# Routing of a mixture of experts: fewer candidate sums, and key numbers picked by compare-and-multiply steps

## What is computed

```python
s1 = einsum('thd,kd->thk', q[:, :, 0], sub_k1)      # scores of 128 keys, first half
s2 = einsum('thd,kd->thk', q[:, :, 1], sub_k2)      # second half
v1, i1 = top_k(s1, 16)
v2, i2 = top_k(s2, 16)
cand = v1[..., :, None] + v2[..., None, :]          # 16 x 16 sums
cand_idx = i1[..., :, None] * 128 + i2[..., None, :]
top_s, top_pos = top_k(cand, 16)
eidx = take_along_axis(cand_idx, top_pos)           # 16 experts of 16384
gate = softmax(top_s)
act = gelu(einsum('thkd,td->thk', expert_u[eidx], x))
y = einsum('thk,thkd->td', gate * act, expert_v[eidx])
```

## Time and profile before

| | us |
|---|---|
| median of 3 runs | 3937.94 |
| the three runs | 3937.94, 3937.79, 3953.55 |
| the profiled execution | 3934.07 |
| its span, from the first to the last instruction | 3932.2 |
| PE busy | 3654.2 |
| DVE busy | 2497.1 |
| POOL busy | 1856.5 |
| ACT busy | 1357.9 |

### The profile page before, as it was taken

One profiled execution on the slowest core, in us unless ns is written; L12 is line 12 of the kernel. 1 busy time (PEld: TensorE's weight loads), 2 busy tenths in 40 slices (PEclk: granted clock), 3 DMA queues, 4 the chain that ended last, 5 costly groups with the idle time before them and its releaser, 6 DMA issues.

```text
span 3932.2 us, 62108 instructions
## 1 busy us (share of the span) xinstructions
PE 3654.2 (93%) x21581; PEld 3445.0 (88%) x21581; DVE 2497.1 (64%) x5088; ACT 1357.9 (35%) x1905; POOL 1856.5 (47%) x1120
## 2 busy tenths in 40 slices
PE   7799999998999999999888599999999999999998
PEld 7799999898999999998853357899898989999998
DVE  2341187878785777775556531287878785777774
ACT  3222244444444333333221233243434444333332
POOL 3333475565555555553520001466555655555551
PEclk9899999999999999999998799999999999999999
DMA  3122266777778999983245131256777788999992
GB/s 119 65 71 75 86 189 221 253 247 256 251 274 274 310 309 318 327 281 99 65 123 174 45 100 49 75 178 215 237 260 240 260 267 294 294 311 318 322 311 101
DMA packets 380008, 812.58 MB, mean 207 GB/s; under 512 B 33544, under 2 KB 239304, under 8 KB 372552
## 3 DMA queue, kind: packets, MB, share of 16 engines
q1 hardware_dynamic: 167024, 464.17, 35.2%
q0 software_dynamic: 61072, 221.08, 16.5%
q10 hardware_dynamic: 151696, 124.51, 10.7%
HBM read 696.90 MB, written 112.74 MB: 206 GB/s over the span
## 4 chain that ended last, share of the span: by engine, by line
PE 68%; DVE 19%; DMA 5%; issue 3%; ACT 2%; POOL 2%; ACTq 0%; SPq 0%; DVEq 0%; POOLq 0%
PE acc L566 39%; PE acc L553 15%; PE misc L697 4%; DMA rows<-u_in,expertP 3%; DVE rows L1626 3%; PE misc L920 2%; DVE hot L1558 1%; DVE hot L1564 1%; POOL w_lo L2039 1%; PE acc L934 1%; DMA raw<-slabs_in 1%; DVE hot_gate L1664 1%; DVE route L1569 1%; DVE work L1521 1%; DVE keyi L1529 1%
## 5 line engine op out<-in xcount | busy, mean ns | idle before, releaser
L2039 POOL TENSOR_TENSOR w_lo<-raw,w_hi 128x1024 fp32r<-128x1024 f32 x368 | 920.1, 2502 | 1349.4 <-ACT w_hi L1015 1348.1
L566 PE MATMUL acc<-h_hi,w_hi 128*128 128x416 f32 x3072 | 1101.5, 359 | 10.4 <-POOL w_lo L2039 9.2
L566 PE MATMUL acc<-h_lo,w_hi 128*128 128x416 f32 x3072 | 1088.6, 354 | 0.0
L566 PE MATMUL acc<-h_hi,w_lo 128*128 128x416 f32 x3072 | 1083.7, 353 | 0.0
L1015 ACT ACTIVATE w_hi<-raw 128x1024 fp32r<-128x1024 f32 x620 | 656.1, 1059 | 1166.1 <-DMA raw<-slabs_in 1134.8
L566 PEld LDWEIGHTS acc<-h_hi,w_hi 128*128 128x128 f32 x3072 | 583.9, 190 | 21.1 <-ACT gelu L1125 11.9
L566 PEld LDWEIGHTS acc<-h_hi,w_lo 128*128 128x128 f32 x3072 | 583.8, 190 | 7.5
L566 PEld LDWEIGHTS acc<-h_lo,w_hi 128*128 128x128 f32 x3072 | 583.5, 190 | 4.2
L1743 DVE TENSOR_TENSOR w_lo<-raw,w_hi 128x1024 fp32r<-128x1024 f32 x252 | 330.8, 1313 | 202.0 <-ACT w_hi L1015 201.6
L1626 DVE CUSTOM_DVE_ANT_0 rows<-acc,rows 128x1024 f32<-128x1024 f32 (+1 forms) x224 | 273.6, 1222 | 226.5 <-DMA rows<-u_in,expertP 182.6
L553 PE MATMUL acc<-h_hi,w_hi 128*128 128x260 f32 x1472 | 308.3, 291 | 78.9 <-DVE h_lo L1433 30.3
(11 more groups left out here) (319 smaller groups left out, 5340.2 us busy)
## 6 DMA issues: line engine op xcount, KB each, us to landing
raw<-slabs_in SPq DMA_DIRECT2D x620, 512.0 KB
act_d<-gelu SPq DMA_DIRECT2D x256, 208.0 KB
gate_d<-gout SPq DMA_DIRECT2D x52, 1024.0 KB
abuf<-act_d ACTq DMA_DIRECT2D x32, 1664.0 KB
gbuf<-gate_d ACTq DMA_DIRECT2D x30, 1664.0 KB
unit<-cv_in SPq DMA_DIRECT2D x128, 128.0 KB, 2.0
unit<-ck_in SPq DMA_DIRECT2D x64, 160.0 KB, 2.9
unit<-ck_in ACTq DMA_DIRECT2D x64, 160.0 KB, 3.2
```

Source lines behind the costliest of these rows:

```text
L566: last = pe.matmul(acc[:, 0, par, 0:ND], w[:, c, :], m(c), start=c == 0 and w is w_hi[r] and m is m_hi, stop=c == KC - 1 and w is w_lo[r])
L2039: pool.tensor_tensor(w_lo[r][:], raw[r][:], w_hi[r][:].bitcast(F32), ALU.subtract).then_inc(lo_done, 1)
```

## The change

Of the 256 sums of a sorted list of 16 with a sorted list of 16, the greatest 16 have either their first place or their second below 4. So 112 sums are kept: the first 4 keys of side one with all 16 of side two (64), and the other 12 with the first 4 (48). They are made by two additions. The place in this list no longer gives the two key places by a shift and a mask, so they are worked out by arithmetic on small float tiles (`rowf`, with five rows in place of two). The key numbers were picked by comparing with 0 to 15, multiplying and summing over 2048 elements for each side; now for each k of 0 to 15 one instruction compares the places with k and multiplies with the number of key k, for both sides in one, and an addition sums it up. The places and the partial picks lie in PSUM (`misc` banks 3 and 2) for the prompt blocks and in SBUF for the sample tokens. `between()` is still called 12 times.

```diff
+EDGE = 4
+PAIRS = EDGE * TOPK + (TOPK - EDGE) * EDGE
...
-        cand = at("cand", [P, PH, TOPK, TOPK], F32, sc_at)
-        cwork = at("cwork", [P, PH, TOPK * TOPK], F32, work_at)
-        hot = at("hot", [P, PH, TOPK, TOPK], F32, work_at)
+        cand = at("cand", [P, PH, PAIRS], F32, sc_at)
+        cwork = at("cwork", [P, PH, PAIRS], F32, work_at)
...
-                dve.tensor_copy(kf[0:w], ki[0:w]).then_inc(dve_step, step.up())
+                dve.tensor_copy(kf[0:w].rearrange("p (s h) k -> p s h k", s=2),
+                                ki[0:w].rearrange("p (h s) k -> p s h k", s=2)).then_inc(dve_step, step.up())
...
-                dve.tensor_tensor(sums[0:w], best[:, 0].unsqueeze(3).to_broadcast([w, heads, TOPK, TOPK]),
-                                  best[:, 1].unsqueeze(2).to_broadcast([w, heads, TOPK, TOPK]), ALU.add).then_inc(
-                    dve_step, step.up())
+                for lo, hi, n, first in ((0, EDGE, TOPK, 0), (EDGE, TOPK, EDGE, EDGE * TOPK)):
+                    each = [w, heads, hi - lo, n]
+                    dve.tensor_tensor(sums[0:w, :, first:first + (hi - lo) * n].rearrange("p h (a b) -> p h a b", b=n),
+                                      best[:, 0, :, lo:hi].unsqueeze(3).to_broadcast(each),
+                                      best[:, 1, :, 0:n].unsqueeze(2).to_broadcast(each), ALU.add).then_inc(
+                        dve_step, step.up())
...
-                dve.tensor_scalar(rw[0:w, 1], tp[0:w], 15, None, ALU.bitwise_and).then_inc(dve_step, step.up())
+                dve.tensor_scalar(rw[0:w, 1], tp[0:w], 2, None, ALU.logical_shift_right).then_inc(dve_step, step.up())
+                dve.tensor_copy(rwf[0:w, 2], tp[0:w]).then_inc(dve_step, step.up())
                 dve.wait_ge(dve_step, step.at)
-                dve.tensor_copy(rwf[0:w], rw[0:w]).then_inc(dve_step, step.up())
+                dve.tensor_copy(rwf[0:w, 0:2], rw[0:w]).then_inc(dve_step, step.up())
                 dve.wait_ge(dve_step, step.at)
-                numbers = kf[0:w].rearrange("p (h s) k -> p s h k", s=2)
-                for s in range(2):
-
-                    dve.tensor_tensor(pick[0:w].rearrange("p h k a -> p (h k) a"),
-                                      rwf[0:w, s].rearrange("p h k -> p (h k)").unsqueeze(2).to_broadcast(
-                                          [w, heads * TOPK, TOPK]),
-                                      iota[0:w, 0:TOPK].unsqueeze(1).to_broadcast([w, heads * TOPK, TOPK]),
-                                      ALU.is_equal).then_inc(dve_step, step.up())
+
+                dve.scalar_tensor_tensor(rwf[0:w, 3], rwf[0:w, 1], float(-(TOPK - EDGE)), rwf[0:w, 0], ALU.add,
+                                         ALU.max).then_inc(dve_step, step.up())
+                dve.wait_ge(dve_step, step.at)
+                dve.tensor_copy(place[0:w, 0], rwf[0:w, 3]).then_inc(dve_step, step.up())
+                dve.scalar_tensor_tensor(rwf[0:w, 0], rwf[0:w, 3], float(-TOPK), rwf[0:w, 2], ALU.mult,
+                                         ALU.add).then_inc(dve_step, step.up())
+                dve.scalar_tensor_tensor(rwf[0:w, 1], rwf[0:w, 3], float(-EDGE), rwf[0:w, 2], ALU.mult,
+                                         ALU.add).then_inc(dve_step, step.up())
+                dve.wait_ge(dve_step, step.at)
+                dve.scalar_tensor_tensor(place[0:w, 1], rwf[0:w, 1], float(-EDGE * (TOPK - EDGE)), rwf[0:w, 0], ALU.add,
+                                         ALU.max).then_inc(dve_step, step.up())
+                dve.wait_ge(dve_step, step.at)
+                between()
+                both = [w, 2 * heads, TOPK]
+                flat = lambda t: t.rearrange("p s h k -> p (s h) k")
+                for k in range(TOPK):
+                    to = flat(pick[0:w] if k else out[0:w, 0:2])
+                    dve.scalar_tensor_tensor(to, flat(place[0:w]), float(k), kf[0:w, :, k:k + 1].to_broadcast(both),
+                                             ALU.is_equal, ALU.mult).then_inc(dve_step, step.up())
                     dve.wait_ge(dve_step, step.at)
-                    dve.tensor_tensor(pick[0:w], pick[0:w],
-                                      numbers[:, s].unsqueeze(2).to_broadcast([w, heads, TOPK, TOPK]),
-                                      ALU.mult).then_inc(dve_step, step.up())
-                    dve.wait_ge(dve_step, step.at)
-                    between()
-                    dve.tensor_reduce(out[0:w, s], pick[0:w], AX, ALU.add).then_inc(dve_step, step.up())
-                    dve.wait_ge(dve_step, step.at)
-                    between()
+                    if k:
+                        dve.tensor_tensor(out[0:w, 0:2], pick[0:w], out[0:w, 0:2], ALU.add).then_inc(dve_step, step.up())
+                        dve.wait_ge(dve_step, step.at)
+                    if k % 6 == 5:
+                        between()
+                between()
...
+            place = misc[:, 3, P:P + 2 * SLOTS].rearrange("p (s h k) -> p s h k", s=2, h=PH)
+            pick = misc[:, 2, 0:2 * SLOTS].rearrange("p (s h k) -> p s h k", s=2, h=PH)
```

More of the change, by code:

```diff
@@ L211, in build @@
         row = take("row", [P, 2, PH, TOPK], U32)
-        rowf = take("rowf", [P, 2, PH, TOPK])
+        rowf = at("rowf", [P, 5, PH, TOPK], F32, work_at + 4096)
         route = take("route", [P, 3, PH, TOPK])
@@ L221, in build @@
         rowS = take("rowS", [P, 2, 1, TOPK], U32)
-        rowfS = take("rowfS", [P, 2, 1, TOPK])
+        rowfS = take("rowfS", [P, 5, 1, TOPK])
         routeS = take("routeS", [P, 3, 1, TOPK])
@@ L245, in build @@
         scS = at("scS", [P, 2, P], F32, s_at)
-        candS = at("candS", [P, 1, TOPK, TOPK], F32, s_at)
+        candS = at("candS", [P, 1, PAIRS], F32, s_at)
         workS = at("workS", [P, 2, P], F32, s_at + 1024)
-        cworkS = at("cworkS", [P, 1, TOPK * TOPK], F32, s_at + 1024)
-        hotS = at("hotS", [P, 1, TOPK, TOPK], F32, s_at + 1024)
+        cworkS = at("cworkS", [P, 1, PAIRS], F32, s_at + 1024)
+        placeS = at("placeS", [P, 2, 1, TOPK], F32, s_at + 1024)
+        pickS = at("pickS", [P, 2, 1, TOPK], F32, s_at + 1536)
         take = region()
@@ L1531, in top16, with chosen @@
                 between()
-            def chosen(w, heads, values, scratch, kv, ki, kf, sums, sums2, tv, tp, td, rw, rwf, pick, out, exp_in,
-                       between):
+            def chosen(w, heads, values, scratch, kv, ki, kf, sums, sums2, tv, tp, td, rw, rwf, place, pick, out,
+                       exp_in, between):
                 top16(lambda k: values[0:w, k, :], lambda k: scratch[0:w, k, :], w, lambda k: kv[0:w, k, :],
                       lambda k: ki[0:w, k, :], 2 * heads, between)
-                dve.tensor_copy(kf[0:w], ki[0:w]).then_inc(dve_step, step.up())
+                dve.tensor_copy(kf[0:w].rearrange("p (s h) k -> p s h k", s=2),
+                                ki[0:w].rearrange("p (h s) k -> p s h k", s=2)).then_inc(dve_step, step.up())
                 best = kv[0:w].rearrange("p (h s) k -> p s h k", s=2)
-                dve.tensor_tensor(sums[0:w], best[:, 0].unsqueeze(3).to_broadcast([w, heads, TOPK, TOPK]),
-                                  best[:, 1].unsqueeze(2).to_broadcast([w, heads, TOPK, TOPK]), ALU.add).then_inc(
-                    dve_step, step.up())
+                for lo, hi, n, first in ((0, EDGE, TOPK, 0), (EDGE, TOPK, EDGE, EDGE * TOPK)):
[4 more added lines that the diff above has]
+                        dve_step, step.up())
                 dve.wait_ge(dve_step, step.at)
-                top16(lambda k: sums[0:w, k].rearrange("p a b -> p (a b)"), lambda k: sums2[0:w, k, :], w,
+                top16(lambda k: sums[0:w, k, :], lambda k: sums2[0:w, k, :], w,
                       lambda k: tv[0:w, k, :], lambda k: tp[0:w, k, :], heads, between)
@@ L1592, in routing @@
                     dve.wait_ge(route_stored, 16 * (l + 1))
-                chosen(P, PH, sc, work, keyv, keyi, keyf, cand, cwork, topv, topp, topd, row, rowf, hot, route,
+                chosen(P, PH, sc, work, keyv, keyi, keyf, cand, cwork, topv, topp, topd, row, rowf, place, pick, route,
                        gate_exp_in, between)
@@ L1600, in sample_routing @@
                 dve.wait_ge(s_sc_taken, l + 1)
-                chosen(SR, 1, scS, workS, keyvS, keyiS, keyfS, candS, cworkS, topvS, toppS, topdS, rowS, rowfS, hotS,
+                chosen(SR, 1, scS, workS, keyvS, keyiS, keyfS, candS, cworkS, topvS, toppS, topdS, rowS, rowfS, placeS, pickS,
                        routeS, s_gate_in, lambda: None)
```

## The result

The changed kernel takes 3902.11 us (median of 4 runs, 3896.54 to 3903.41) against 3940.36 us for the kernel before (4 runs in this comparison): 38 us less, ratio 0.990, interval 0.9883 to 0.9917. I had predicted 3888, with a range of 3873 to 3912. The profiled execution took 3903.41 us. In the profiled pair the step is smaller, 3934.07 to 3903.41 us, since what lies outside phase s happened to take 5 us more in the second. Lines of the kernel are numbered 2 higher than before ahead of `chosen` and 17 to 19 higher behind it: 748 is now 750, 1579 is 1596, 697 is 699, 1664 is 1683, 1626 is 1645.

What follows compares the result with a forecast made beforehand. PE was 93% busy and lost 63 us around eight routing windows waiting for DVE's route. Terms gave 24.2 us a layer, 48.4 for both, plus 1 to 2 for PE's pace, say 50: 3888 against the median 3937.94, range 3873 to 3912.

Steps and rivals of the forecast that it cites:

- (a): In a full routing window, splitting the `cand` add of 2048 elements into adds of 512 and 384 gains 1.1 us.
- (b): In a full routing window, the second `top16` on 112 elements in place of 256 gains 6.0 us.
- (c): In a full window, the longer decode chain takes about 2.3 us in place of 0.93, a loss of 1.4.
- (d): 31 small picks at 0.45 us with wait take 13.9 us a window; gain about 2.9 in blocks 1 to 3, 5.1 in block 0.
- rival B: Small dependent instructions cost more, with two port meetings a window: 23 us gained, 3915, or half of it, 3902; chance 0.2.
- (e): DVE and POOL take turns at the port: picks in PSUM are free, split `cand` or decode may lose 2.4 us.
- (f): The sample's routing in block 0 grows by at most 7.3 us, under a cover of 8.8, so costed at nothing.
- (g): `between()` is still called 12 times, with up to 5.4 us of picks between calls; rows land in time, cost nothing.
- The gain passes on: Step phases behind the windows are paced by PE and DVE stands before their end, so the windows' gain reaches the time.
- rival C: Given back: the route is early but PE stands elsewhere, less than 20 us stay, 3920 to 3945; chance 0.08.
- Rival A: The cap is reached, no POOL instruction between adds or in decode: six windows gain 8.6 us or more, 3875 to 3879; chance 0.2.
- Rival D: Slower: picks run far slower than priced, at 1.0 us each giving 4001; chance 0.04.

## Why the prediction was right, and where its steps were off

I predicted 50 us and measured 38. The result is in the range, outside the forecast's own 3881 to 3900 by 2 us. In phases s, which the sum is about, it is 35.8: PE's windows gave 39.8 of the 48.4 us, and the step phases took 4.0 more. Point by point.

- **The bound.** Right: both waits of the earlier trace rows that were to fall did. PE's wait for the route was to be some 15 us and is 22.6. The cap of 63 us was right: without picks the windows are 63.2 us shorter. What it left out is the step phases, which lost 10.8 us in that kernel and gained 5.0 in the same one with the one-hots first.
- **(a) and (b).** Right in size. MAX8 on 112 elements is 261 ns (0.26 predicted), and the shortest stretch from first dot to `topd` went from 44.1 to 37.2 us (36.9 in the kernel with the one-hots first): 6.9 to 7.2, where the terms were 1.1 + 6.0.
- **(c) Decode.** 2.44 us when free, 2.3 predicted.
- **(d) Picks.** 431 and 424 ns, 14.2 us for 31; predicted 0.42, and 13.9 for all. The fixed latency that rival B took from the Trainium skill ("VectorE: DVE Perf Modes", The TRN2 errata) weighed no more than in my sum. The gain was somewhat less than priced: free of meetings, `topd` to the route went from 23.2 to 22.2 us in blocks 1 and 2, 1.0 in place of 2.9 - 1.4 = 1.5.
- **(e) The port.** The rule was right for the picks, and what rests on it, that picks in PSUM are free, is shown: 14.2 us in every window, and in SBUF 62 us lost. It was too narrow for the rest: I counted only steps with two inputs in SBUF, but casts, with one input, met POOL too. The cast of the key numbers, 0.29 us when free, took 0.60 to 1.86 in six of eight windows (0.57 to 1.57 in five of them before), and the decode's cast 3.10 in the lines above. The second half of (e) failed in place, and somewhat in size. I put a meeting on the second sum in blocks 0 and 1 and on the decode in block 3. Measured: the second sum in both blocks 0 and in block 1 of layer 0 (2.74 to 2.75 us, as said), but in layer 1 in block 2 and not in block 1; the decode in block 2 of layer 0 (6.1 us) and block 1 of layer 1 (4.5), where I had put nothing, and hardly in block 3 (2.9 and 2.6). In block 3 of layer 0 the stretch ahead of `topd` lost 2.8 instead, 2.2 of it at `hS`, which my list of exposed steps didn't have. Against 59.1 us, a window without a meeting (36.9 + 2.4 + 19.8), the six windows lost 2.4 to 4.6 us, 3.4 in the mean; the kernel before lost 1.1 in the mean against its own 67.3 (44.1 + 23.2). That is 2.3 more a window; I had priced 2.4, 0.9 and 2.4, 1.9 in the mean. A phase between two engines, read from a trace of the kernel before, doesn't hold in a kernel in which both run otherwise; the rate of meetings would have been the thing to price.
- **(f) The sample's routing** was to take 7.3 us more at the most and took 8.7: DVE begins block 0's own routing at 506.75 in place of 499.54, in an execution whose phase s began 1.46 us earlier (PE's first score at 483.86 in place of 485.32). The 31 steps of 0.18 us lie in SBUF, and three of them and the step behind met the four `w_lo` of that stretch. DVE, then POOL:

```profile
491.44 2.33 DVE L1580 SCALAR_TENSOR_TENSOR pickS<-placeS,keyfS 64x32 f32<-64x32 f32 x1
...
495.76 2.39 DVE L1580 SCALAR_TENSOR_TENSOR pickS<-placeS,keyfS 64x32 f32<-64x32 f32 x1
...
499.06 2.29 DVE L1584 TENSOR_TENSOR routeS<-pickS,routeS 64x32 f32<-64x32 f32 x1
...
504.43 2.39 DVE L1622 SCALAR_TENSOR_TENSOR expertS<-routeS 64x16 uint32<-64x16 f32 x1
```

```profile
491.33 2.40 POOL L2058 TENSOR_TENSOR w_lo<-raw,w_hi 128x1024 fp32r<-128x1024 f32 x1 [13.08 <-ACT w_hi L1017]
495.73 2.38 POOL L2058 TENSOR_TENSOR w_lo<-raw,w_hi 128x1024 fp32r<-128x1024 f32 x1 [2.00 <-ACT w_hi L1017]
498.90 2.41 POOL L2058 TENSOR_TENSOR w_lo<-raw,w_hi 128x1024 fp32r<-128x1024 f32 x1 [0.79 <-ACT w_hi L1017]
504.40 2.40 POOL L2058 TENSOR_TENSOR w_lo<-raw,w_hi 128x1024 fp32r<-128x1024 f32 x1 [3.09 <-ACT w_hi L1017]
```

  I had worked out the port for the full window and not for this form. The cover of 8.8 us was used up: POOL's first fetch now waits for DVE's `expertS`.

```profile
507.11 1.05 POOL L2101 DMA_INDIRECT rows<-u_in,expertS  x1 [0.32 <-DVE expertS L1622]
```

  The first dot is still 28.93 us behind PE's first score, as before, and its wait 2.67 us in place of 11.3. That the term could be put at nothing held by some 0.1 us, which is luck: one more meeting would have moved the window.
- **(g)** Right within the window: no dot but the first waits for its rows in blocks 0 to 3.
- **The sum.** Measured on PE, from scores to route, the eight windows gained 39.8 us of my 48.4: block 0 3.9 each (3.7 predicted), the six others 32.0 in place of 41.0. This is the larger part of what was missing. Of these 9 us the smaller free gain is 3 (8.1 in place of 8.6 a window), the meetings are 2.4, and in layer 0's block 1 the first dot came 20.9 us after PE's first score in place of 18.5, another 2.4; 1.2 are spread.
- **"The gain passes on."** This is the step whose argument failed. I argued that the step phases are paced by PE because DVE stands at their end. It does stand there, but its order of work inside the phase put dots without rows ahead of what PE wants, and 26 us of that loss were there before the change. What the change itself gave back is small: 4.0 us by the step phases before and after, 2.1 by the two pairs of kernels; in block 3's stage alone 2.5 a layer. This is rival C's mechanism, at about an eighth of the 30 us that C needed.

With the one-hots first the change is worth 46 us, 4 short of the 50, but most of what this is above 38 lies in the windows and not in the closed leak. Of rival B, the price of small steps fell flat (431 and 424 ns), and its meetings came to 3.4 us a window where it had 4.8. Rival A's gain of 8.6 us was reached in none of its six windows (4.0 to 8.0). Rival D needed picks at twice their price; only with the picks in SBUF did the kernel become slower, by the port and not by the instruction.

What stays open: how much of the windows' rest could be had. The kernel freed of the port in its small steps still met POOL in four of six windows, and where a meeting falls depends on the phase between DVE and POOL, which I could move but not set. Why the turned order takes 26 us off the step phases of the kernel before, where PE's named waits for the one-hots sum to 13.2, was not taken apart. And how much the step phases vary from one execution to the next was not measured: each kernel has one profile.

## What to carry to other kernels

When many small instructions take the place of a few large ones, look first at where their operands lie: here 31 small steps a window brought 14 us with an operand in PSUM, and with all of them in SBUF the same steps, as fast when free, cost 62 us more. When work ahead of a phase gets shorter, read what the engine does next in its own order: whatever waits for a transfer must stand behind what another engine waits for, else the time won is spent standing. Turning two lines of that order round gave 28 us here, where the whole change gave 38.

## What the runs showed of the hardware that I had not expected

- A GpSimd elementwise instruction gets in between two DVE instructions with two SBUF inputs even where DVE would otherwise run them back to back, without a wait between them: the second sum, of 384 elements, took 2.74 to 2.76 us in four of eight windows in place of 0.55.
- Being short doesn't protect: a step of 64 partitions by 32 elements, 0.18 us when free, took 2.29 to 2.39 us in each of three meetings in one stretch, the whole of the other's instruction. A cast of 256 elements, with a single input, was held up alike (3.10 us in place of 0.29).
- The fetch of rows on POOL, 0.95 us in the median, took 1.76 us when it began beside the long sum of DVE at 647.71 in the kernel freed of the port, and 2.83 us at 684.73 in the kernel before, beside a multiply of 2048 elements: on POOL the issue of a transfer can be lengthened too.
